# Feed-forwards of a network of ten stages: inner up tiles as a wide and a narrow pass per product, root scaling on GpSimd

## The reference, cut to what matters

```
h = rmsnorm(x) * gain
u = depthwise_conv3(h @ w_up) + bias        # w_up: 1024 x 5632; 3 taps along the 256 positions
y = (gelu(gate half of u) * value half of u) @ w_down      # w_down: 2816 x 1024
x = x + y                                   # ffn0: x + rmsnorm(y) * gain
```

## Time and profile before

| what | value |
| --- | --- |
| median of 3 runs | 1634.12 us (1634.01 to 1635.59) |
| the profiled execution's own time | 1633.69 us |
| its span, first to last instruction | 1631.9 us |
| outside the span | 1.8 us |
| feed-forward 0 in the span | about 146 to 334 us, of which the loop of pairs is 170 to 323 us |

### The profile page before, as it was taken

The page is one execution under the profiler, slowest core; times in us unless marked ns, Lnnn a source line. Parts: engine busy times, 40 slices in busy tenths (PEclk is TensorE's granted clock), DMA queues, the critical chain, the costliest instruction groups (busy, mean ns, idle before and its releaser), DMA issues.

```text
span 1631.9 us, 28614 instructions
## 1 busy us (share of the span) xinstructions
PE 1608.2 (99%) x10556; PEld 1459.0 (89%) x10556; DVE 1221.7 (75%) x1841; ACT 902.6 (55%) x1188; POOL 93.0 (6%) x93
## 2 busy tenths in 40 slices
PE   9999999999999999999999999999999999999998
PEld 8888999978899999888999998878999987899997
DVE  5756877778787877875878786456787887878787
ACT  5476554565655446675554555444645556664543
POOL 0041000000000001320000033000100000000000
PEclk9999999999999999999999999999999999999999
DMA  7444545443654554422545455534554455345453
GB/s 289 141 144 167 206 172 193 174 161 124 254 191 174 183 202 150 161 104 104 206 170 194 176 187 195 186 129 142 182 200 184 180 180 181 134 154 207 176 181 128
DMA packets 41618, 284.15 MB, mean 174 GB/s; under 512 B 4976, under 2 KB 5104, under 8 KB 8656
## 3 DMA queue, kind: packets, MB, share of 16 engines
q1 hardware_dynamic: 39280, 273.90, 45.9%
q0 software_dynamic: 2272, 9.32, 1.6%
HBM read 282.16 MB, written 1.05 MB: 174 GB/s over the span
## 4 chain that ended last, share of the span: by engine, by line
PE 87%; DVE 8%; ACT 2%; issue 2%; DMA 0%; POOL 0%; DVEq 0%; SPq 0%; ACTq 0%
PE bank L1897 15%; PE bank L1899 14%; PE bank L1898 14%; PE bank L1995 8%; PE bank L1996 8%; PE bank L1997 8%; PE bank L1945 4%; PE bank L1947 4%; PE bank L1946 4%; DVE w_lo L1083 2%; DVE arena L1370 1%; PE bank L2056 1%; PE bank L1879 1%; PE bank L2333 1%; PE bank L2043 1%
## 5 line engine op out<-in xcount | busy, mean ns | idle before, releaser
L1897 PE MATMUL bank<-h_hi,w_hi 128*128 128x256 f32 x2220 | 633.5, 285 | 5.8 <-issue 2.3
L1898 PE MATMUL bank<-h_hi,w_lo 128*128 128x256 f32 x2220 | 630.2, 284 | 0.0
L1899 PE MATMUL bank<-h_lo,w_hi 128*128 128x256 f32 x2220 | 630.2, 284 | 0.0
L1897 PEld LDWEIGHTS bank<-h_hi,w_hi 128*128 128x128 f32 x2220 | 425.5, 192 | 12.5 <-issue 4.8
L1898 PEld LDWEIGHTS bank<-h_hi,w_lo 128*128 128x128 f32 x2220 | 425.6, 192 | 3.2
L1899 PEld LDWEIGHTS bank<-h_lo,w_hi 128*128 128x128 f32 x2220 | 425.6, 192 | 0.8
L1397 DVE TENSOR_TENSOR w_lo<-raw,w_hi 128x2048 fp32r<-128x2048 f32 x145 | 327.6, 2285 | 1.6 <-ACT w_hi L819 1.6
L807 ACT ACTIVATE arena<-arena,par 128x256 f32<-128x256 f32 x220 | 120.4, 595 | 357.9 <-DVE arena L1356 354.7
L1083 DVE TENSOR_TENSOR w_lo<-raw,w_hi 128x2048 fp32r<-128x2048 f32 (+3 forms) x109 | 235.0, 2157 | 107.0 <-ACT w_hi L605 107.0
L819 ACT ACTIVATE w_hi<-raw 128x2048 fp32r<-128x2048 f32 x150 | 286.1, 1907 | 19.7 <-PE bank L1997 19.7
L1995 PE MATMUL bank<-w_hi,h_hi 128*128 128x512 f32 x632 | 248.2, 393 | 1.5 <-DVE h_lo L1391 1.5
(11 more groups left out here) (216 smaller groups left out, 1361.0 us busy)
## 6 DMA issues: line engine op xcount, KB each, us to landing
raw<-wstream SPq DMA_DIRECT2D x254, 1024.0 KB, 4.8
arena<-window_bias POOLq DMA_DIRECT2D x4, 768.0 KB, 7.7
arena<-dilated_bias POOLq DMA_DIRECT2D x8, 256.0 KB, 4.9
arena<-conv_rows POOLq DMA_DIRECT2D x2, 1024.0 KB, 4.9
raw<-wstream SPq DMA_DIRECT2D x6, 256.0 KB, 3.3
raw<-wstream SPq DMA_DIRECT2D x4, 384.0 KB, 3.5
cst<-consts SPq DMA_DIRECT2D x1, 1088.0 KB, 14.8
x<-x_in SPq DMA_DIRECT2D x1, 1024.0 KB, 5.1
```

The lines of the kernel that those rows point to most:

```text
L1897: nc.tensor.matmul(dst, w_parts[0], x_parts[0], start=start, stop=False, **kw)
L1898: nc.tensor.matmul(dst, w_parts[1], x_parts[0], start=False, stop=False, **kw)
L1899: return nc.tensor.matmul(dst, w_parts[0], x_parts[1], start=False, stop=stop, **kw)
```

## The change

Tiles 2 to 19 of each feed-forward (18 of 22) get another form. For each of their 16 products TensorE loads the high weights once and passes 512 columns over them, high and low activations side by side, and then loads the low weights and passes the 256 high columns. The high-by-low sum thus lies in columns of its own: a tile's gate and value halves take two banks of 512 (`up_bank[a]`), and two such pairs of banks alternate where three banks rotated. The bank of the statistics (`bank[7]`) is now one of them, so the root row of a feed-forward goes to bank 3.

ScalarE copies the high-by-low halves to SBUF (`high_by_low`), VectorE adds them to the rest (`up_sums`), and GpSimd multiplies the sum by the roots (in `up_n`). Tiles 0, 1, 20 and 21 keep three passes and `up_norm`. In VectorE's queue the split of down i-1 moves from ahead of tile 2i's reading to behind the parts of 2i-1; in ScalarE's queue the split of the next chunk moves ahead of `centre`. The last pair leaves the loops.

```
+        h_both = sb("h_both", [P, 32, S], F32R)
+        h_hi, h_lo = h_both[:, 0:16, :], h_both[:, 16:32, :]
+        both_parts = h_both[:, :, :].rearrange("p (a t) s -> p t a s", a=2)
...
+        up_bank = [ctx.enter_context(nc.psum_tensor(f"bank{i}", [P, 2, 512], F32)) for i in range(2)]
+        bank = [up_bank[0][:, 0, :], up_bank[0][:, 1, :], up_bank[1][:, 0, :]]
+        bank += [ctx.enter_context(nc.psum_tensor(f"bank{i}", [P, 512], F32)) for i in range(3, 7)]
+        bank.append(up_bank[1][:, 1, :])
...
+        corr, up_sum = region(A0, 2, 512), region(A0 + 1024, 2, 512)
+        DUAL = FT - 4
...
+                if name.startswith("ffn"):
+                    T0, U0 = k["ffn"] * FT, k["ffn"] * DUAL
+                    for t in range(2, FT - 2):
+                        pool.wait_ge(up_summed, U0 + t - 1)
+                        pool.wait_ge(taps_done, 4 * T0 + 4 * t - 4)
+                        nc.gpsimd.tensor_tensor(halves(up_n[:, t % 2, :]), halves(up_sum[:, t % 2, :]),
+                                                rs_row[:, :].unsqueeze(1).broadcast_to([P, 2, S]), ALU.mult).then_inc(up_ready, 1)
...
+                def high_by_low(t, a, used):
+                    act.wait_ge(chunk_used, used)
+                    nc.scalar.activation(halves(corr[:, a, :]), up_bank[a][:, :, S:2 * S], ACT.Copy).then_inc(corr_ready, 1)
...
-                with act.Fori(1, FT // 2) as i:
+                with act.Fori(1, FT // 2 - 1) as i:
                     loop_split(i, 0)
                     for a in range(2):
+                        high_by_low(i * 2 + a, a, i * 3 + (c0 + a))
+                        loop_split(i, 1 + a)
                         centre(i * 2 + a, a)
-                        loop_split(i, 1 + a)
                         gelu(i * 2 + a, a)
...
+                def up_sums(t, a):
+                    dve.wait_ge(corr_ready, t + (U0 - 1))
+                    nc.vector.tensor_tensor(halves(up_sum[:, a, :]), up_bank[a][:, :, 0:S], halves(corr[:, a, :]), ALU.add)\
+                             .then_inc(up_summed, 1)
...
-                def two_tiles(i):
+                def two_tiles(i, dual=True):
                     used = i * 3 + (c0 - 1)
                     parts(i * 2 + (-2), 0, used)
-                    if not isinstance(i, int):
+                    if not isinstance(i, int) or i > 1:
                         loop_split(i, -1)
-                    loop_split(i, 0)
-                    up_norm(i * 2, 0, (c0 + 2) % 3, i * 3 + c0)
+                    if dual:
+                        up_sums(i * 2, 0)
+                    else:
+                        up_norm(i * 2, 0, i * 3 + c0)
                     gated_value(i * 2 + (-1), 1)
                     parts(i * 2 + (-1), 1, used)
+                    loop_split(i, 0)
                     taps(i * 2, 0)
-                    up_norm(i * 2 + 1, 1, (c0 + 3) % 3, i * 3 + (c0 + 1))
+                    if dual:
+                        up_sums(i * 2 + 1, 1)
+                    else:
+                        up_norm(i * 2 + 1, 1, i * 3 + (c0 + 1))
                     loop_split(i, 1)
                     gated_value(i * 2, 0)
                     taps(i * 2 + 1, 1)
...
+                def dual(t, a, c, slot_c):
+                    pe.wait_ge(lo_done, c + 1)
+                    if isinstance(t, int) and t < 4:
                         pe.wait_ge(up_ready, t + (T0 - 1))
+                    else:
+                        pe.wait_ge(up_summed, t + (U0 - 3))
                     for m in range(2):
                         for kt in range(8):
+                            hi, lo = weights(slot_c, (8 * m + kt) * P)
+                            nc.tensor.matmul(halves(up_bank[a][:, m, :]), hi, both_parts[:, kt, :, :], start=kt == 0, stop=False,
+                                             skip_group_check=True)
+                            last = nc.tensor.matmul(up_bank[a][:, m, 0:S], lo, h_hi[:, kt, :], start=False, stop=kt == 7,
+                                                    skip_group_check=True)
                     last.then_inc(chunk_used, 1)
...
+                up(0, 0, c0, c0, wait_h=k["hlo"])
+                up(1, 1, c0 + 1, c0 + 1, between=lambda: root_row(bank[DOWN0]))
+                dual(2, 0, c0 + 2, c0 + 2)
+                dual(3, 1, c0 + 3, c0 + 3)
                 down(0, c0 + 4, c0 + 4, first=True)
-                with pe.Fori(2, FT // 2) as i:
+                with pe.Fori(2, FT // 2 - 1) as i:
                     for a in range(2):
-                        up(i * 2 + a, i * 3 + (c0 - 1 + a), c0 + 2 + a)
+                        dual(i * 2 + a, a, i * 3 + (c0 - 1 + a), c0 + 2 + a)
                     down(i - 1, i * 3 + (c0 + 1), c0 + 4)
+                i = FT // 2 - 1
+                for a in range(2):
+                    up(i * 2 + a, a, i * 3 + (c0 - 1 + a), c0 + 2 + a)
+                down(i - 1, i * 3 + (c0 + 1), c0 + 4)
```

More of the change, by code:

```diff
@@ L244, in build_program @@
         arena = sb("arena", [P, ARENA])
-        bank = [ctx.enter_context(nc.psum_tensor(f"bank{i}", [P, 512], F32)) for i in range(8)]
+        up_bank = [ctx.enter_context(nc.psum_tensor(f"bank{i}", [P, 2, 512], F32)) for i in range(2)]
+        bank = [up_bank[0][:, 0, :], up_bank[0][:, 1, :], up_bank[1][:, 0, :]]
+        bank += [ctx.enter_context(nc.psum_tensor(f"bank{i}", [P, 512], F32)) for i in range(3, 7)]
+        bank.append(up_bank[1][:, 1, :])
         stat = bank[7]
@@ L262, in build_program @@
         root_diag, row_sum, row_done = sem("root_diag"), sem("row_sum"), sem("row_done")
-        up_ready = sem("up_ready")
+        up_ready, corr_ready, up_summed = sem("up_ready"), sem("corr_ready"), sem("up_summed")
         wide_half = sem("wide_half")
@@ L692, in x_squares, with prenorm @@
                     nc.scalar.activation(xs_piece(q), x_piece(q), ACT.Square, accum_out=sum_at(q)).then_inc(piece_sq, 1)
-            def prenorm(c0, gain, by_row=True, then=None):
+            def prenorm(c0, gain, by_row=True, then=None, row_bank=stat):
                 if c0:
@@ L729, in prenorm @@
                 act.wait_ge(row_sum, k["row"])
-                nc.scalar.activation(rs_row[:, :], stat[:, 0:S], ACT.Copy).then_inc(row_done, 1)
+                nc.scalar.activation(rs_row[:, :], row_bank[:, 0:S], ACT.Copy).then_inc(row_done, 1)
             def post(c):
@@ L826, in ffn @@
                 gelu(1, 1)
-                with act.Fori(1, FT // 2) as i:
+                with act.Fori(1, FT // 2 - 1) as i:
                     loop_split(i, 0)
                     for a in range(2):
+                        high_by_low(i * 2 + a, a, i * 3 + (c0 + a))
+                        loop_split(i, 1 + a)
                         centre(i * 2 + a, a)
-                        loop_split(i, 1 + a)
                         gelu(i * 2 + a, a)
+                i = FT // 2 - 1
+                loop_split(i, 0)
+                for a in range(2):
+                    centre(i * 2 + a, a)
+                    loop_split(i, 1 + a)
+                    gelu(i * 2 + a, a)
                 split_hi(c0 + 34)
@@ L847, in _ @@
                     then = lambda: tables_of(ACT.Silu)
-                prenorm(c0, lambda t: pcol(*pre_gain(name, t)), not name.startswith("conv"), then)
+                prenorm(c0, lambda t: pcol(*pre_gain(name, t)), not name.startswith("conv"), then,
+                        bank[DOWN0] if name.startswith("ffn") else stat)
                 if name == "mix":
@@ L1355, in up_norm @@
                         dve.wait_ge(taps_done, t * 4 + (4 * T0 - 4))
-                    nc.vector.tensor_tensor(halves(up_n[:, a, :]), halves(bank[bank_][:, :]),
+                    nc.vector.tensor_tensor(halves(up_n[:, a, :]), up_bank[a][:, :, 0:S],
                                             rs_row[:, :].unsqueeze(1).broadcast_to([P, 2, S]), ALU.mult).then_inc(up_ready, 1)
@@ L1400, in ffn @@
                 prenorm(gain, c0)
-                up_norm(0, 0, c0 % 3, c0 + 1)
-                up_norm(1, 1, (c0 + 1) % 3, c0 + 2)
+                up_norm(0, 0, c0 + 1)
+                up_norm(1, 1, c0 + 2)
                 taps(0, 0)
@@ L1423, in ffn @@
                 two_tiles(1)
-                with dve.Fori(2, FT // 2) as i:
+                with dve.Fori(2, FT // 2 - 1) as i:
                     two_tiles(i)
+                two_tiles(FT // 2 - 1, dual=False)
                 parts(FT - 2, 0)
@@ L1885, in keep_busy, with root_row @@
                     nc.tensor.transpose(unused[:, 0:P], ident, ident)
-            def root_row():
+            def root_row(row_bank=stat):
                 k["row"] += 1
@@ L1892, in root_row @@
                     pe.wait_ge(stat_read, k["stat"])
-                nc.tensor.matmul(stat[:, 0:S], ones, hn[:, 0, :], start=True, stop=True).then_inc(row_sum, 1)
+                nc.tensor.matmul(row_bank[:, 0:S], ones, hn[:, 0, :], start=True, stop=True).then_inc(row_sum, 1)
```

(42 more changed lines are left out.)

8 lines of the change are left out of this document (4 added, 4 removed).

## The result

The changed kernel takes **1666.91 us** (median of 4 runs, 1666.06 to 1667.46), the kernel before 1634.07 us beside it: a ratio of 1.0201, 95% interval 1.0190 to 1.0213, or 32.8 us more. The forecast was 1666 us.

A forecast was written before the change was run, and what follows sets the result against it. TensorE was taken to bound the kernel before; longer chain and VectorE's holds add 6.55 us per feed-forward, five times +32.8, to the profiled 1633.69 us: 1666.5 us, likeliest 1666. Range 1618 to 1680.

The forecast's parts named there:

- What bounds the kernel: Kernel before: TensorE bounds the loop, pair and down chunk 16.98 us without waits; VectorE next, over 3.5 us idle.
- The hold: VectorE and reading GpSimd block each other: GpSimd ends 1.15 us behind a split; VectorE's cast held until about x+2.05.
- Rival B: At GpSimd's multiplications only GpSimd waits, VectorE isn't held: 17.01 us a pair, 1640 us; chance 0.13.
- C: GpSimd and VectorE don't meet, TensorE bounds every pair at 16.60 us: faster, 1620 us; chance 0.20.
- D: GpSimd gets the port only when VectorE waits: a pair takes some 19.4 us, about 1735 us; chance 0.05.
- The pair: Two inner tiles with down chunk: 17.5 us against 16.98, from 35.0 us for two pairs through VectorE and TensorE.
- The start and the end of feed-forward 0: First down chunk at 171.33 (+1.18), last loop chunk 311.63 (+5.64), down chunk 9 at 329.52 us (+6.55).
- TensorE's saving: Inner tiles' products: 0.3478 us instead of 0.3598, a tile 5.565 instead of 5.76; 17 us over five feed-forwards.
- the prediction's formula: Two pairs: 7.28 us from first to second sum, 10.11 to the odd split's end, 17.62 back through TensorE.
- The cover: VectorE's idle time, over 3.5 us of each 16.98 us pair, is what the change draws on.

The follow-up runs named there:

- e1: The changed kernel, but GpSimd fills the tile with a constant, reading nothing in SBUF, instead of multiplying the sum by the roots: 1626.71 us, ratio 0.9958.
- e5: The changed kernel with only TensorE's wide and narrow passes: no copy, sum or GpSimd, old order, high-by-low sums left out: 1625.19 us, ratio 0.9948.
- e10: The kernel before, plus a GpSimd multiplication of a constant table by itself (512 columns) that nobody waits for: 1633.70 us, ratio 0.9999.
- e6: e5, but the wide pass reads 512 neighbouring columns in SBUF instead of two runs of 256 lying 16 KB apart: 1625.10 us, ratio 0.9947.
- e8: e5 with the two passes of each product in the other order, narrow first: 1625.42 us, ratio 0.9946.

## Why the prediction was right, and where it was not

- **What bounds the kernel**: right. TensorE's spacings were the bound before, and in the changed kernel VectorE's splits end TensorE's waits.
- **The hold**: right in mechanism and size, for both sides of it. GpSimd ends 1.16 us behind the split it waited for (1.15 said), gets in between two VectorE instructions back to back, and VectorE is held 0.98 us at the cast and 1.10 at the gated product (about 1.0 said). The prediction left open whether a cast is held; it is. Rival B (VectorE not held) falls with the 1.27 and 1.52 us rows, C (no meeting) with all 90 multiplications, of which the quickest took 1.40 us and the mean one 2.34 (1.27 alone); D (GpSimd starved) with the 254.27 row.
- **The pair**: 17.5 said, 17.52 measured in feed-forward 0 and 17.59 over all five, and by the way predicted, through both engines in two periods: the alternation 17.92 and 17.15 is a cycle of 35.07 us (35.0 said).
- **The start and the end of feed-forward 0**: 171.33, 311.63 and 329.52 us said, 171.41, 311.58 and 329.57 measured. Of this 0.2 us is already there at its first tile, so the steps' errors are below 0.3 us. The prediction took it five times; the other four cost more, since their odd splits end 10.18 to 10.25 us behind the second sum, not 10.07 as in feed-forward 0. Most of that lies between GpSimd's end and `centre` at the odd tiles: 0.24 us in feed-forward 0, 0.32 to 0.42 in the others, but for one of 0.61. Why is open. The profiled executions differ by 33.7 us, 0.9 more than said.
- **TensorE's saving**: twice too large. The step "I take the mean spacings of both widths" gave 0.3478 us a product; four tiles in five take 0.353. A tile saves 0.11 us, not 0.19, and all of them 8.5 us where 17 were named. Case C's 1620 us was wrong by the same term: e1 and e5 put it at 1625 to 1627.
- **Luck in the number**: with 5.645 us a tile the prediction's formula gives (7.28 + 10.11 + 17.78)/2 = 17.59 a pair, 0.08 more than it said and some 3 us over forty pairs. The sum hardly noticed, because two latencies were too large by as much. The second sum comes 7.15 us behind the first, not 7.28, mostly because ScalarE's copy starts 0.33 us behind the start of the gelu, where its whole 0.42 was counted, and the odd split ends at 10.07, not 10.11. With these the formula gives 17.50, and 17.52 was measured in feed-forward 0. That the total is within 1 us of the measured one is in part this cancelling.
- **The cover**: the prediction let the change draw on over 3.5 us of VectorE's idle time and walked through one pair what is left of it. That was right: the idle time pays for most of a hold alone (e10) and for a chain with a short step on GpSimd (e1), but not for both together.

## What to carry to other kernels

Idle time of the second-busiest engine is cover once, for everything that a change lays on it: holds, moved work and longer latencies have to be walked through one period together, and where a period's end feeds the next through two engines, through two periods. An elementwise step moved to GpSimd isn't free for VectorE when both read SBUF; here VectorE was held for 1.0 us in place of 0.6 us of its own work. And a longer chain should begin where the pipeline has slack, not in its first turn.

## What the runs showed of the hardware that was not expected

A pass of 512 columns and one of 256 in alternation take 0.353 us together in most tiles and 0.347 in some (16 of 90 in the changed kernel), where passes of their own kind take 0.228 and 0.120; neither the place of the columns in SBUF nor the order of the two makes the usual pace faster (11.29 to 11.31 us for 32 products in e5, e6 and e8). The Trainium skill (TensorE: Matmul & The Clock Gate, "Wait — 56ns, not 53.3ns?") gives 2.5 ns of fixed cost per pass; here it is 13 to 17 ns (by those spacings less the columns at 2.4 GHz).

The cast of 256 columns, 0.29 us alone, is held by GpSimd's reading about as long as the gated product with its two inputs is (0.98 and 1.10 us). By the Trainium skill (SBUF — State Buffer, "Who interferes with whom") casts can take both ports, and the trace agrees with its 1.27 us.
